# Expert gates: one-hot products on TensorE replaced by additions into a zeroed table in device memory

## The reference

```
q = (xn @ w_pq)                      # 8 heads x 256
s1, s2 = q[:128] @ sub_k1.T, q[128:] @ sub_k2.T
v1, i1 = top_k(s1, 16); v2, i2 = top_k(s2, 16)
vs, ci = top_k(all sums v1 + v2, 16)
eid = i1[ci // 16] * 128 + i2[ci % 16]      # one of 16384 experts
g = softmax(vs)                             # over the 16 of a head
a = gelu(xn . u_tab[eid])
out = sum over the 128 chosen experts of (a * g) * v_tab[eid]
```

## Time and profile before

| | us |
|---|---|
| median of 3 runs | 3982.46 |
| lowest and highest | 3979.25, 3983.03 |
| span of the profiled execution, first to last instruction | 3974.8 |
| PE busy | 3931.7 (99%) |
| DVE busy | 2423.6 (61%) |
| ACT busy | 2005.7 (50%) |
| POOL busy | 69.8 (2%) |

### The profile page before, as it was taken

The page is one execution under the profiler, slowest core; times in us unless marked ns, Lnnn a source line. Parts: engine busy times, 40 slices in busy tenths (PEclk is TensorE's granted clock), DMA queues, the critical chain, the costliest instruction groups (busy, mean ns, idle before and its releaser), DMA issues.

```text
span 3974.8 us, 82642 instructions
## 1 busy us (share of the span) xinstructions
PE 3931.7 (99%) x33899; PEld 3890.2 (98%) x33899; DVE 2423.6 (61%) x3562; ACT 2005.7 (50%) x3047; POOL 69.8 (2%) x74
## 2 busy tenths in 40 slices
PE   8999999999999999999999999999999999999998
PEld 8999999999999999999999999999999999999998
DVE  7655565575555556555666667987755555555555
ACT  7555554454444444455554554457754444444443
POOL 2000000000000000000000000000000000000000
PEclk9999999999999999999999999999999999999999
DMA  5545555555555555444335544555555556665553
GB/s 212 181 164 177 177 174 193 197 184 193 196 191 190 192 196 189 170 167 149 130 128 191 180 170 152 189 191 178 184 201 190 191 195 217 211 213 190 196 193 127
DMA packets 111189, 726.09 MB, mean 183 GB/s; under 512 B 11296, under 2 KB 11424, under 8 KB 29184
## 3 DMA queue, kind: packets, MB, share of 16 engines
q1 hardware_dynamic: 105904, 701.55, 51.4%
q0 software_dynamic: 5072, 21.50, 1.7%
HBM read 712.52 MB, written 10.49 MB: 182 GB/s over the span
## 4 chain that ended last, share of the span: by engine, by line
PE 89%; DVE 6%; ACT 3%; issue 1%; DMA 0%; DVEq 0%; SPq 0%; ACTq 0%
PE ps L522 17%; PE ps L530 17%; PE ps L523 17%; PE ps L611 9%; PE ps L618 9%; PE ps L613 9%; DVE wl L1814 3%; ACT oh_g L1721 1%; ACT wh L1157 1%; PE ps L578 1%; PE ps L583 1%; PE ps L684 1%; PE ps L579 1%; DVE oh_g L2665 1%; PE ps L703 1%
## 5 line engine op out<-in xcount | busy, mean ns | idle before, releaser
L1814 DVE TENSOR_TENSOR wl<-raw,wh 128x1024 fp32r<-128x1024 f32 x1328 | 1622.9, 1230 | 1361.2 <-ACT wh L1157 1355.2
L1157 ACT ACTIVATE wh<-raw 128x1024 fp32r<-128x1024 f32 x1328 | 1402.4, 1060 | 1772.0 <-PE ps L611 599.1
L522 PE MATMUL ps<-x,wh 128*128 128x256 f32 x6560 | 1554.5, 279 | 1.6 <-ACT qt L1249 1.0
L523 PE MATMUL ps<-x,wh 128*128 128x256 f32 x6560 | 1540.5, 277 | 0.0
L522 PEld LDWEIGHTS ps<-x,wh 128*128 128x128 f32 x6560 | 1233.9, 188 | 8.8 <-issue 6.1
L523 PEld LDWEIGHTS ps<-x,wh 128*128 128x128 f32 x6560 | 1233.9, 188 | 0.5
L530 PE MATMUL ps<-x,wl 128*128 128x256 f32 x6560 | 884.0, 277 | 0.3 <-DVE wl L1814 0.3
L530 PEld LDWEIGHTS ps<-x,wl 128*128 128x128 f32 x6560 | 810.7, 188 | 0.5 <-DVE wl L1814 0.5
L611 PE MATMUL ps<-xkh,wh 128*128 128x256 f32 x3328 | 776.2, 276 | 3.1 <-DVE xkl L1825 1.9
L613 PE MATMUL ps<-xkl,wh 128*128 128x256 f32 x3328 | 775.4, 276 | 0.0
L611 PEld LDWEIGHTS ps<-xkh,wh 128*128 128x128 f32 x3328 | 624.8, 188 | 4.7 <-DVE xkl L1825 2.9
(11 more groups left out here) (396 smaller groups left out, 2457.8 us busy)
## 6 DMA issues: line engine op xcount, KB each, us to landing
raw<-in_w_in SPq DMA_DIRECT2D x184, 1024.0 KB, 4.8
raw<-in_expert_u SPq DMA_DIRECT2D x128, 1024.0 KB, 4.8
raw<-in_expert_v SPq DMA_DIRECT2D x128, 1024.0 KB, 4.8
raw<-in_w_ffn_gate SPq DMA_DIRECT2D x44, 1024.0 KB, 4.7
raw<-in_w_ffn_up SPq DMA_DIRECT2D x44, 1024.0 KB, 4.8
raw<-in_w_ffn_down SPq DMA_DIRECT2D x44, 1024.0 KB, 4.7
raw<-in_w_out SPq DMA_DIRECT2D x32, 1024.0 KB, 4.8
raw<-in_w_branch SPq DMA_DIRECT2D x16, 1024.0 KB, 5.0
```

The costliest lines, as they stand in the source:

```text
L522: begin(mm(o, wh[:, j, c], x_h[:, kc, :], start=kc == 0, stop=False), kc % 8 == 0)
L523: mm(o, wh[:, j, c], x_l[:, kc, :], start=False, stop=False)
L1157: f(wh[:, u % 4, 0:width], raw[:, ring, c:c + width], ACT.Copy).then_inc(*k.up("hi"))
L1814: v.tensor_tensor(wl[:, u % 4, 0:width], raw[:, ring, c:c + width], wh[:, u % 4, 0:width].bitcast(F32), ALU.subtract).then_inc(*k.up("lo"))
```

## The change

Gates are no longer made by products. A table `gates` of 128 x 128 x 256 floats (16 MB: expert row, expert column, token) lies in device memory. GpSimd writes zeros into it, in 16 transfers of 1 MB, each after the one before has landed, between `masks_free` and the masks of the second block.

When a head's experts are found, DVE works out each one's place in the table and writes it to `gidx` as integers (three more operations at the end of part 7). For two heads at a time DVE asks ACT for the exponentials (`weights_asked`, `weights`) and normalises them two tiles later (`weights_normed`). ACT does this at tiles 0, 8, 18 and 28 of u0. GpSimd then issues, for each head, 2 x 16 indirect transfers; each adds 128 weights, one for each partition (token), into the table. It waits for the 32 of a head before the next head's.

The one-hot sets, their products, the transposes, the two-piece gelu and `awake` are gone. In u0 ACT writes plain gelus for all 64 tiles. At c = 61 DVE waits for the first four rows of gates (`g0_in`) and multiplies them into `ag`; the first two rows of v0 are split at c = 63. In v0 GpSimd loads the gates of four rows (512 KB) at a time into slot 0 of `gbuf`, and DVE multiplies them in, four rows ahead of every four rows; ACT waits for that (`gated`) before the split of the third row of a turn. u1 reads the upper half in 16 loads of four rows into four slots.

```diff
--- before.py
+++ after.py
...
+PEER_HEADS = 8
+HEADS_AT_ONCE = 2
...
         ag = at("ag", 0, [P, HALF, T])
-        e1t = rstd
-        e2t = at("e2t", 64, [P, T])
-        g_t = at("g_t", 65, [P, T])
-        oh_l = at("oh_l", 66, [P, 2, 4, P])
-        oh_g = at("oh_g", 70, [P, 2, 4, P])
-        stage = at("stage", 74, [P, 2, HALF, 16])
-        gt_row = nc.alloc_sbuf_tensor_at("gt_row", [P, 2, T], F32, offset=xk0)
-        gbuf = at("gbuf", 64, [P, 2, 16, P])
+        gbuf = at("gbuf", 64, [P, 4, 4, T])
+        gidx = at("gidx", 79, [P, PEER_HEADS, 2, TOPK], I32)
         gt3 = at("gt3", 80, [P, 2, T])
-        g1 = nc.dram_tensor("g1", (16, P, HALF * 16), F32, kind="Internal").ap()
+        zeros = at("zeros", 70, [P, T])
+        gates = nc.dram_tensor("gates", (N_KEYS * P * T, 1), F32, kind="Internal").ap()
+        gate_rows = gates.rearrange("(e p t) o -> e p (t o)", e=N_KEYS, p=P)
...
-        ROUTE_ROW = 32
         MEM_SQUARES = 12
+        WEIGHT_TILES = (0, 8, 18, 28)
...
-            def route(n):
-
-                b = 2 + n % 4
-                pe.wait_ge(*k.next("oh_ready"))
-                pe.wait_ge(*k.next("lr_ready"))
-                reserve(b)
-                for s in range(4):
-                    m = mm(ps[:, b, s * P:(s + 1) * P], oh_l[:, n % 2, s, :], oh_g[:, n % 2, s, :], start=True, stop=True)
-                    if s == 2:
-                        m.then_inc(*k.up(f"full_a{b}"))
-                m.then_inc(*k.up(f"full_v{b}"))
-                marks["route", n] = k.n[f"full_v{b}"]
-
...
-                if c == ROUTE_ROW - 2:
-                    pe.wait_ge(*k.next("idx_ready"))
-                    for n, src in enumerate((etab[:, :, 0, :], etab[:, :, 1, :], wts[:])):
-                        reserve(3 + n)
-                        for i in range(2):
-                            m = nc.tensor.transpose(ps[:, 3 + n, i * P:(i + 1) * P], src[:, i, :], ident[:])
-                        m.then_inc(*k.up(f"full_v{3 + n}"))
-                if c >= ROUTE_ROW:
-                    for t in range(2):
-                        route(2 * (c - ROUTE_ROW) + t)
-            awake(24, 7)
             residual("v0", HALF)
...
+            def residual(src, name, n, more=True, between=None, early=False, gated=False):
                 act.wait_ge(*k.next("src_ready"))
+                if gated:
+                    act.wait_ge(*k.next("gated"))
...
                             split()
+                            if gated and j == 2:
+                                act.wait_ge(*k.next("gated"))
                             xsplit(src, i * 4 + (2 + j), k.at("hi", -3))
...
-            def weigh_hots(n):
...
-            def stage_out(n):
...
-            for c in range(ROUTE_ROW):
+            def weights(turn):
+                c = slice(turn * HEADS_AT_ONCE * TOPK, (turn + 1) * HEADS_AT_ONCE * TOPK)
+                act.wait_ge(*k.next("top_m"))
+                f(wts[:, :, c], wts[:, :, c], ACT.Exp).then_inc(*k.up("top_e"))
+            for c in range(HALF):
                 b = c % 2
+                if c == HALF - 1:
+                    early_rows(ag)
                 done(b)
                 f(ag[:, c, :], ps[:, b, 0:T], ACT.Gelu_apprx_tanh).then_inc(*k.up(f"free_a{b}"))
                 if c == 0:
                     keys_out(7)
-                if c == ROUTE_ROW - 3:
-                    act.wait_ge(*k.next("top_m"))
-                    f(wts[:], wts[:], ACT.Exp).then_inc(*k.up("top_e"))
-            flag("a_ready")
-            weigh_hots(0)
-            weigh_hots(1)
-            for c in range(ROUTE_ROW, HALF):
-                i, b = c - ROUTE_ROW, c % 2
-                t = 8 * (i + 1)
-                done(b)
-                act.wait_ge(*k.next("gate_free"))
-                f(gt_row[:, b, 0:t], ps[:, b, 0:t], ACT.Gelu_apprx_tanh).then_inc(*k.up("act" if t < T else f"free_a{b}"))
-                if t < T:
-                    f(ag[:, c, t:T], ps[:, b, t:T], ACT.Gelu_apprx_tanh).then_inc(*k.up(f"free_a{b}"))
-                flag("gate_ready")
-                for n in (2 * i, 2 * i + 1):
-                    stage_out(n)
-                    if n + 2 < 64:
-                        weigh_hots(n + 2)
-            residual(ag, "v0", HALF)
+                if c in WEIGHT_TILES:
+                    weights(WEIGHT_TILES.index(c))
+            residual(ag, "v0", HALF, early=True, gated=True)
             for q in range(4):
                 act.wait_ge(*k.next("h_ready"))
             split(True)
-            for turn in range(2):
-                act.wait_ge(S[f"g1_out{turn}"], 16 * 8)
...
                     with k.loop(name, dve, n // 4 - 1) as i:
+                        if group is not None:
+                            group(i * 4 + 4)
...
+                    c = slice(h * TOPK, (h + 1) * TOPK)
                     for i in range(2):
-                        v.tensor_reduce(etab[:, i, :, h * TOPK:(h + 1) * TOPK], grid(eqb[:])[:, 2 * i:2 * i + 2],
+                        v.tensor_reduce(etab[:, i, :, c], grid(eqb[:])[:, 2 * i:2 * i + 2],
                                         AX.X, ALU.add).then_inc(*k.up("dve"))
                     own()
-            def one_hots(n):
...
-            def weigh(n, rows):
...
+                    token = iota[:, TOPK:TOPK + 2].unsqueeze(2).to_broadcast([P, 2, TOPK])
+                    place = cijf[:, :, 0, :]
+                    step(v.scalar_tensor_tensor(place, etab[:, :, 1, c], float(T), token, ALU.mult, ALU.add))
+                    step(v.scalar_tensor_tensor(place, etab[:, :, 0, c], float(P * T), place, ALU.mult, ALU.add))
+                    step(v.tensor_copy(gidx[:, h], place))
+            def weights_asked(turn):
+                flag("top_m")
+            def weights_normed(turn):
+                c = slice(turn * HEADS_AT_ONCE * TOPK, (turn + 1) * HEADS_AT_ONCE * TOPK)
+                rows = wts[:, :, c].rearrange("p i (h s) -> p i h s", s=TOPK)
+                total = small[:, 20:24].rearrange("p (i h) -> p i h", i=2)
+                dve.wait_ge(*k.next("top_e"))
+                step(v.tensor_reduce(total, rows, AX.X, ALU.add))
+                step(v.reciprocal(small[:, 20:24], small[:, 20:24]))
+                v.tensor_tensor(rows, rows, total.unsqueeze(3).to_broadcast([P, 2, HEADS_AT_ONCE, TOPK]),
+                                ALU.mult).then_inc(*k.up("idx_ready"))
+            def gate_group(first):
+                dve.wait_ge(*k.next("g0_in", 16))
+                a = ag[:, bass.ds(first, 4), :]
+                v.tensor_tensor(a, a, gbuf[:, 0], ALU.mult).then_inc(*k.up("gated"))
 
...
+                if c == 13:
+                    weights_asked(0)
+            for c in range(HALF):
+                if c == HALF - 1:
+                    half()
+                    early_rows(ag)
+                    half()
+                else:
+                    split()
+                if c < 28:
                     searches(c + 12)
-                elif c == ROUTE_ROW - 4:
-                    flag("top_m")
-                elif c == ROUTE_ROW - 3:
-                    dve.wait_ge(*k.next("top_e"))
-                    for i in range(2):
-                        row = wts[:, i, :].rearrange("p (h s) -> p h s", s=TOPK)
-                        total = small[:, 20 + 8 * i:28 + 8 * i]
-                        step(v.tensor_reduce(total, row, AX.X, ALU.add))
-                        step(v.reciprocal(total, total))
-                        step(v.tensor_tensor(row, row, total.unsqueeze(2).to_broadcast([P, 8, TOPK]), ALU.mult))
-                    flag("idx_ready")
-                elif c == ROUTE_ROW - 1:
-                    for n, dst in enumerate((e1t, e2t, g_t)):
-                        take(3 + n)
-                        v.tensor_copy(dst[:], ps[:, 3 + n, 0:T]).then_inc(*k.up(f"free_v{3 + n}"))
-                    own()
-                    one_hots(0)
-                    one_hots(1)
-            dve.wait_ge(*k.next("a_ready"))
+                if c in WEIGHT_TILES:
+                    if c:
+                        weights_asked(WEIGHT_TILES.index(c))
+                elif c - 2 in WEIGHT_TILES:
+                    weights_normed(WEIGHT_TILES.index(c - 2))
+                if c == HALF - 3:
+                    gate_group(0)
+                    flag("early_ready")
             for b in range(2):
                 flag("gate_free")
-            for c in range(ROUTE_ROW, HALF):
-                i = c - ROUTE_ROW
-                t = 8 * (i + 1)
-                split()
-                for n in (2 * i, 2 * i + 1):
-                    weigh(n, c)
-                    if n + 2 < 64:
-                        one_hots(n + 2)
-                dve.wait_ge(*k.next("gate_ready"))
-                own()
-                v.tensor_tensor(ag[:, c, 0:t], ag[:, c, 0:t], gt_row[:, c % 2, 0:t], ALU.mult).then_inc(*k.up("gate_free"))
-            for b in range(2):
-                flag("gbuf_free")
```

(45 more changed lines are left out.)

53 lines of the change are left out of this document (12 added, 41 removed), and 1 row of the table LOOP_COUNTS.

## The result

| | before | after |
|---|---|---|
| median of the runs | 3980.99 us (3979.25 to 3983.03, 4 runs) | 4136.31 us (4134.12 to 4140.34, 4 runs) |
| span of the profiled execution | 3974.8 | 4132.4 |
| TensorE busy | 3931.7 (99%) | 3872.2 (94%) |
| GpSimd busy | 69.8 | 529.5 |
| ratio of the times | | 1.0389, interval 1.0376 to 1.0403 |

The forecast was 3921 us, faster. What came is rival A, with an addition at about 2.0 us: 4131 by the prediction's formula. The median also lies above the range's upper end of 4110.

What follows compares the result with a forecast made beforehand. TensorE, busy 99% at full clock, was taken to bound the kernel: span 3974.8 - 67.3 (products removed) + 6 (DVE's search work) = 3913.5; from the median, 3982.5 - 67.3 + 6 = 3921 us. Range 3911 to 3930; 8 in 10 reaches to 4110.

Steps and rivals of the forecast that it cites:

- rival A: Additions on GpSimd over 1.18 us each, TensorE idle before v0, kernel slower; 4131 at 2.0 us each; chance 0.35.
- the prediction's formula: Time if additions are late before v0: 3921 + 256 (a - 1.18), a being us for one addition.
- the price of one addition: GpSimd's time for one indirect addition in u0: taken as 1.15 us, so that all 256 are hidden.
- the limit of 1.18: Most us per addition that fits: 302 us left for 256 between tile 2 of u0 and about 2836.
- the landings and the way from the last one to TensorE: Eight landings between heads of some 2.5 us; last landing at about 2836, v0's first row at 2846.6.
- the 7.7 us that the prediction carries from the span to the time: Whole kernel: median of the runs lies 7.7 us above the profiled span, assumed unchanged after.
- The bounds were 0.53 to 3.4: Range for one addition on GpSimd: 0.53 us like a store's issue, 3.4 with a landing each.
- -67.3 us on TensorE: Between tile 30 and v0's first product: 248.7 us become 181.4 as gate products, transposes and idle ones go.
- +6 us by DVE in the search stage: Up to tile 27 of u0: DVE's new work exceeds its lead, TensorE waits 6 us, bounds 0 and 11.
- the sum of three costs: DVE in u0: places 4.1, normalising 2.1, asking for exponentials 5.6 us; 11.8 against a lead of 4.1.
- Zeroing, v0 and u1 at 0: Zero transfers at 8.6 + 1.15 us each, v0's multiplications and loads, and u1 cost TensorE nothing.
- Rival D: Small pieces slow the weight stream over 60 tiles, 34 us lost, 3955; chance 0.12 together with another rival.

Runs made afterwards that it cites:

- f4: Changed kernel with its 256 indirect transfers storing their words instead of adding them: 4186.97 us (one run).
- g1: Changed kernel with each of the 256 indirect additions replaced by a direct addition at a fixed place, without indices: 3922.31 us (one run).
- i1: g1 with the sum left out, so 256 direct stores of 128 words at fixed places: 3922.09 us (one run).
- g3: f1 with the exponentials taken one tile later on ACT and their sums one tile later on DVE: 3916.56 us (one run).
- f1: Changed kernel without the 256 indirect additions, all else done: 3917.57 us (3914.68 to 3921.96, 4 runs), ratio to before 0.9833.
- h1: Changed kernel reordered: scores of all 128 expert tiles first, then one residual over all value rows: 3918.01 us (5 runs), ratio to before 0.9849.

## Why the prediction was wrong

- **The step that failed** is the price of one addition: "for the indices I go up to the dearest issue seen and take 1.15, which fits by 8 us". It is 2.01. 256 x (2.01 - 1.18) = 213 us, and the prediction's formula with this value gives 3921 + 213 = 4134; 4136.3 was measured. The mechanism, the limit of 1.18 and rival A's slope held; the branch was chosen by a row of another kind of instruction.
- **How near 4134 is.** In part by luck. The first addition was forecast at 2513.5 and came at 2520.3 (2.4 of the 6.8 us were lost before the experts start), and the clock's return after the wait costs 2.4 (below). Against that, the landings and the way from the last one to TensorE took 2.3 less, and of the 7.7 us that the prediction carries from the span to the time only 1.7 came (4134.12 - 4132.4). Together 4135 for the profiled execution's 4134.1; the median is 2.2 above it.
- **How the choice was wrong.** The bounds were 0.53 to 3.4 and the limit lay at 1.18, in the lower quarter of them. "By number of pieces it is nearest to the store" took pieces for the cost. Runs f4, g1 and i1 show four terms instead: 0.54 for the 128 pieces, which the earlier trace rows had; 0.32 for adding; 0.69 for the indices of an addition; and 0.30 behind each. That is 1.85, and 0.17 by DVE makes 2.01. A cost estimated by the nearest row of another form, that decides with a margin of 8 us in 302, deserved a chance near a half, not 0.35.
- **What the bounds missed**: an issue on GpSimd can be lengthened by DVE. This is 439.9 - 256 x 1.55 = 43 us of the 532, all of it in the covered part.
- **The rule of the Trainium skill** that was set beside the forecast (page "DMA: Bandwidth & Descriptors", section "Anatomy of one DMA": about 2.0 us fixed for a GpSimd DMA, whatever it moves) named 4131, the right total, by coincidence. Read as a price that adds up it isn't right here: a direct store of the same 128 words is issued in 0.54 and the next one follows at once, so the 2.01 is the sum of the terms above. As a warning against 256 small transfers it was worth more than the row that I followed.
- **-67.3 us on TensorE**: right. From the last product with the keys to v0's first product it is 411.3 us before and 344.0 in g3, which has no wait in between: 67.3 less. f1 is 3917.6 where the sum was 3921.
- **+6 us by DVE in the search stage**: 4.5 measured. From the last product with the keys to the end of the gelu of tile 62 it is 344.1 us in the changed kernel and 339.6 in g3. The waits themselves are 3.6 of it (2.46 near 2609 and 1.39 near 2667, each less a product's pitch of 0.11). The size was near but the path wasn't the forecast one: the prediction let DVE's late `wl` stop TensorE, by the sum of three costs. What stopped it was ACT's late gelu, since ACT stood at DVE's flag, and with the ask a tile apart nothing of it is left.
- **Zeroing, v0 and u1 at 0**: right. The zero transfers landed in 6.1 us (8.6 taken) and TensorE lost nothing there (busy for 179.9 of 180 us from 820 to 1000, before and after); the loads of 512 KB were issued in 0.75 and landed in 5.3.
- **Rival D**, small pieces that slow the weights: no. In u0 the weights landed in 5.0 us beside 128 pieces every 2 us, and in 5.1 beside twice as many in g1.

## What to carry to other kernels

When a change puts a serial chain on an engine that was idle, the chain's length is its count times the price of one, and the time is free only while something covers it: work out the limit per item first, and if the trace has no row of that very instruction, measure 128 of them by themselves before building on it. Of the price, the number of pieces is only a part (0.54 us of 1.85 here); indices from a table cost 0.42 to 0.69 and another 0.30 behind the issue, a sum in memory 0.32 to 0.59. When the chain turns out too long, look for work that doesn't depend on it and put it in between: here an order of stages was worth 218 us, with no instruction of the chain made cheaper.

## What the runs showed of the hardware that I hadn't expected

- An indirect issue of GpSimd that meets a running `wl` of DVE is held until about its end (up to 1.0 us longer, beside `wl` of 1.23), and not the other way round. The two fall into step, so the mean issue from 2675 to 2836 us is 1.88 with tiles of 5.44 us and 1.60 with tiles of 5.65.
- Indirect stores of 128 single words, one every 1.27 us, bring the whole core nearly to a stop for stretches: products of TensorE 0.7 to 2.8 us apart and the weight stream at 0 GB/s. Indirect additions (every 2.0 us), direct additions (every 0.89) and direct stores don't. The packets don't tell the ways apart: about 32 for a store and 145 for an addition, with indices and without (6432 for 198 direct stores from 2540 to 2700 us). What stops the core, and whether it depends on the pace, stays open.
- After 216 us of waiting TensorE's granted clock was 0.50 (1.2 GHz), and v0's first 20 products or so came 0.213 us apart (3064.13 to 3064.34 above) instead of 0.11, until 3068.4, 2.4 us in all, before it was back at 2.4 GHz. TensorE was idle from 2847.7. In f1 a much shorter wait, 2.2 us, was followed by 3.4 us at 0.50 (16 products, 1.6 us lost); in the changed kernel and in h1 one of the same length wasn't. The stretch in the stall, columns as above:

```profile
2860.00:3050.00 190.00, 0.00 (x0) 0.00 (x0) 0.00 (x0) 0.00 (x0) 155.36 (x101) 0.50 0.22 0
```
